# Where the weight tiles of a float32 matmul kernel begin in SBUF, modulo 64 bytes

## What is computed

```python
def _swiglu(h, w_gate, w_up, w_down):
    return (jax.nn.silu(h @ w_gate) * (h @ w_up)) @ w_down

proj = jnp.einsum("bld,de->ble", h, w_in)               # first block, 1024 x 7168
conv_out = jnp.einsum("blc,cd->bld", cu * silu(z_c), w_conv_out)
...
for layer in range(2):
    x = x + 0.5 * _swiglu(_rmsnorm(x, g[0]), ...)       # w_gate, w_up 1024 x 2816
    h = _rmsnorm(x, g[1])
    mix = conv_rwkv_mixer(h, ...) if layer == 0 else mla_mixer(h, ...)
    x = x + mix
    x = x + 0.5 * _swiglu(_rmsnorm(x, g[2]), ...)       # w_down 2816 x 1024
```

## The kernel before, in words

| tiles | begin, modulo 64, before |
|---|---|
| `w_raw`, `w_hi`, `w_lo`, `xT`, `R`, `par`, `ident`, `ones`, `bones` | 0 |
| `gu_w_hi1`, `gu_w2` with `gu_w_lo2` (over the ring) | 0 |
| `gu_w_hi0`, `gu_w0`/`gu_w_lo0`, `gu_w1`/`gu_w_lo1` (in the arena) | 32 |
| all moving tiles of the large products, `tmp`, `st_hi`, `st_lo` | 32 |

## Time and profile before

### The profile page before, as it was taken

How to read it: one execution, slowest core, us unless ns; L and a number is a source line. 1 busy time by engine, 2 the same in 40 slices (tenths; PEclk the granted TensorE clock), 3 DMA queues, 4 the chain that set the end, 5 groups by cost and what they waited for, 6 DMA issues and landing times.

```text
span 2443.8 us, 42260 instructions
## 1 busy us (share of the span) xinstructions
PE 2379.5 (97%) x16963; PEld 2001.1 (82%) x16963; DVE 1738.9 (71%) x2296; ACT 1148.6 (47%) x1758; POOL 879.2 (36%) x533
## 2 busy tenths in 40 slices
PE   8999999999999999989999999999999999999999
PEld 6666767789899777877998998998987557898997
DVE  6999986496485589766864867855846676883771
ACT  5533353465364346244652645643644344662552
POOL 3799934322313456422123123132134212114123
PEclk9999999999999999999999999999999999999999
DMA  5222224233343432002434342342423221333333
GB/s 149 78 78 78 74 65 130 60 93 104 99 111 84 112 93 67 27 4 57 121 84 115 104 121 78 92 124 79 111 85 98 51 57 53 87 94 108 102 89 94
DMA packets 420791, 214.48 MB, mean 88 GB/s; under 512 B 17317, under 2 KB 419035, under 8 KB 420603
## 3 DMA queue, kind: packets, MB, share of 16 engines
q1 hardware_dynamic: 416523, 209.05, 31.1%
q10 hardware_dynamic: 4080, 2.83, 0.5%
HBM read 209.22 MB, written 2.10 MB: 86 GB/s over the span
## 4 chain that ended last, share of the span: by engine, by line
PE 85%; DVE 9%; ACT 3%; issue 2%; POOL 1%; DMA 0%; ACTq 0%; DVEq 0%; POOLq 0%
PE bank L337 11%; PE bank L334 11%; PE bank L330 11%; PE bank L987 11%; PE bank L992 10%; PE bank L995 10%; PE bank L1848 3%; PE bank L1852 3%; PE bank L1855 3%; DVE bank L1682 3%; PE bank L3392 1%; PE bank L2740 1%; PE bank L3458 1%; DVE hL L361 1%; PE bank L2720 1%
## 5 line engine op out<-in xcount | busy, mean ns | idle before, releaser
L312 POOL TENSOR_TENSOR w_lo<-w_raw,w_hi 128x1024 fp32r<-128x1024 f32 (+5 forms) x276 | 532.4, 1931 | 631.9 <-ACT w_hi L304 630.2
L304 ACT ACTIVATE w_hi<-w_raw 128x1024 fp32r<-128x1024 f32 (+5 forms) x276 | 237.7, 861 | 649.0 <-PE bank L337 486.4
L584 DVE TENSOR_TENSOR gu_w_lo<-gu_w,gu_w_hi 128x1024 fp32r<-128x1024 f32 (+1 forms) x256 | 365.2, 1429 | 99.6 <-ACT gu_w_hi L575 99.0
L656 POOL TENSOR_TENSOR ffn_aL<-tmp,ffn_aH 128x512 fp32r<-128x512 f32 x88 | 134.6, 1529 | 739.5 <-ACT ffn_aH L700 739.5
L575 ACT ACTIVATE gu_w_hi<-gu_w 128x1024 fp32r<-128x1024 f32 (+1 forms) x256 | 303.2, 1186 | 3.0 <-DVE gu_w L558 3.0
L692 ACT ACTIVATE tmp<-bank 128x256 f32<-128x256 f32 x320 | 121.6, 380 | 191.0 <-PE bank L995 187.5
L987 PE MATMUL bank<-hH,gu_w_hi 128*128 128x256 f32 x1280 | 205.1, 282 | 4.8 <-ACT tmp L692 4.8
L992 PE MATMUL bank<-hL,gu_w_hi 128*128 128x256 f32 x1280 | 204.0, 282 | 0.0
L995 PE MATMUL bank<-hH,gu_w_lo 128*128 128x256 f32 x1280 | 204.0, 282 | 0.0
L960 DVE TENSOR_TENSOR bank<-bank,R 128x512 f32<-128x512 f32 x64 | 44.8, 699 | 212.9 <-PE bank L337 212.0
L330 PE MATMUL bank<-ffn_aH,w_hi 128*128 128x512 f32 x704 | 185.2, 395 | 0.0
(11 more groups left out here) (553 smaller groups left out, 4707.7 us busy)
## 6 DMA issues: line engine op xcount, KB each, us to landing
gu_w<-in_ffn_w_gate SPq DMA_DIRECT2D x88, 512.0 KB, 4.0
gu_w<-in_ffn_w_up SPq DMA_DIRECT2D x88, 512.0 KB, 5.3
w_raw<-in_w_in SPq DMA_DIRECT2D x48, 512.0 KB, 3.8
w_raw<-in_ffn_w_down SPq DMA_DIRECT2D x64, 384.0 KB, 3.4
w_raw<-in_ffn_w_down SPq DMA_DIRECT2D x64, 320.0 KB, 3.2
w_raw<-in_even_w_in SPq DMA_DIRECT2D x26, 512.0 KB, 3.8
w_raw<-in_w_conv_out SPq DMA_DIRECT2D x8, 512.0 KB, 3.8
w_raw<-in_w_out SPq DMA_DIRECT2D x8, 512.0 KB, 3.8
```

The source lines that it names most:

```text
L304: nc.scalar.activation(w_hi[u % 2][:, 0:K, :], w_raw[u % 4][:, 0:K, :], ACT.Identity).then_inc(w_hi_ready, 1)
L312: nc.gpsimd.tensor_tensor(w_lo[u % 2][:, 0:K, :], w_raw[u % 4][:, 0:K, :], w_hi[u % 2][:, 0:K, :].bitcast(F32), ALU.subtract).then_inc(w_l ...
L584: nc.vector.tensor_tensor(gu_wl[v % 3][:, b0:b1, :, :], gu_w[v % 3][:, b0:b1, :, :], gu_wh[v % 2][:, b0:b1, :, :].bitcast(F32), ALU.subtra ...
L656: nc.gpsimd.tensor_tensor(aL[:, in_half(n), :], up_t[:, :], aH[:, in_half(n), :].bitcast(F32), ALU.subtract).then_inc(a_lo, 1)
```

## The change

Layout only. The 32-byte tile `small` moves to the front, so that `xT`, the ring, `R`, `par` and the constants begin 32 bytes past a multiple of 64; `tmp`, `hH`, `hL` and the arena stay where they were. The gate and up buffers in the arena are moved on by 32 bytes with a new method `skip`, and those laid over the ring begin 32 bytes behind its start, so that all five begin on multiples of 64; `ffn_aH` and `ffn_aL` move by 64 bytes, the `st_` tiles by 128. Shapes, streams of instructions, waits and DMAs are the same.

```diff
@@ -90,11 +90,16 @@
+            def skip(self, n):
+                self.at += n
+                return self.at
+
 ...
         m = Map(base0)
+        small = m.put("small", [P, 8])
         xT = m.put("xT", [P, DT, T])
         ring_at = m.at
 ...
         bones = m.put("bones", [P, P])
-        small = m.put("small", [P, 8])
         tmp = [m.put(f"tmp{i}", [P, T]) for i in range(6)]
@@ -395,15 +399,17 @@
         f_map = Map(ARENA)
-        u_at = [f_map.at, 0, ring_at]
+        u_at = [f_map.skip(32), 0, ring_at + 32]
         f_map.put("gu_room0", [P, 7, 4, P])
+        f_map.skip(32)
         aH = f_map.put("ffn_aH", [P, GU, T], F32R)
         aL = f_map.put("ffn_aL", [P, GU, T], F32R)
-        u_at[1] = f_map.at
+        u_at[1] = f_map.skip(32)
         f_map.put("gu_room1", [P, 7, 4, P])
         gu_w = [Map(at).put(f"gu_w{i}", [P, 7, 4, P]) for i, at in enumerate(u_at)]
         gu_wl = [Map(at).put(f"gu_w_lo{i}", [P, 7, 4, P], F32R) for i, at in enumerate(u_at)]
-        gu_wh = [f_map.put("gu_w_hi0", [P, 7, 4, P], F32R), Map(ring_hi_at).put("gu_w_hi1", [P, 7, 4, P], F32R)]
+        gu_wh = [f_map.put("gu_w_hi0", [P, 7, 4, P], F32R), Map(ring_hi_at + 32).put("gu_w_hi1", [P, 7, 4, P], F32R)]
+        f_map.skip(32)
```

## The result

The changed kernel takes 2431.68 us (median of 4 runs, 2430.86 to 2434.25) where the kernel before, in the 4 runs it has by now, takes 2445.80. The ratio is 0.9942 (95% interval 0.9930 to 0.9954). So it is faster, as forecast, but by 14.1 us and not by 35, and the time lies above the range of 2400 to 2424 us.

What follows compares the result with a forecast made beforehand. TensorE, busy 97% of the span, was taken as the bound. Ring 26.4 plus gate and up 12.1, less plain units 1.8 and waits 1.5, gave 35.2 us: 2443.8 - 35.2 = 2408.6 us, range 2400 to 2424.

Steps and rivals of the forecast that it cites:

- That TensorE bounds, and that a start address sets its spacing: Whole kernel: TensorE, busy 97% of the span, is the bound, and where its weights lie sets a matmul's time.
- The rule for the spacing: Weights at 32 modulo 64 cost 6.6 ns less than at 0 for 512 columns; for 256 columns the sign turns.
- Down halves: Ring units of the eight down halves, 512 columns: 59.8 instead of 61.6 us each, 13.9 us gained.
- The first rival: Down matmuls stay at 233.3 ns if the pair must agree modulo 128: 2422.5 us; 0.10, shared with other missing gains.
- Gate and up: The 80 units of 256 columns, weights moved to 0 modulo 64: all take 9.81 us, 12.1 us gained.
- The third rival: New gate and up residues make the kernel slower, up to 2473.7 us if a bad pair adds 6.6 ns; chance 0.05.
- Ring outside the down halves, less the waits: First block and mixers, ring at 32 modulo 64: 12.5 us gained, 1.5 taken off for waits, 11.0 together.
- Pair loop worth nothing, other engines worth nothing: First block's pair loop, where VectorE never rests, and other engines' tiles with new residues: zero taken for each.
- Plain units: Eight units of 512 columns: 272 matmuls have weights moved from 32 to 0, 1.8 us lost.
- The second rival: Memory region of the weight buffers, ring or arena, sets the rate, so nothing changes: 2443.8 us; chance 0.09.
- The rule against the change: TensorE's two independent read ports never wait, so spacing cannot hang on start addresses; the gain would be zero.
- Nothing has to be carried over: Whole kernel: profiled span 2443.8 us and median run 2443.76 agree, so a sum against the span needs no adjustment.

Runs made afterwards that it cites:

- bare loop: Kernel's work replaced by rows of 32 fp32r matmuls at varied weight and moving-tile starts, nothing else running: 226.7 to 234.3 ns (512 columns), 113.3 to 120.2 (256).
- ring alone: Kernel before with only the ring tiles moved, to 160 modulo 256; gate and up buffers and moving tiles keep their places: 2425.17 us, ratio 0.9922.
- gate and up alone: Changed kernel with the ring back at 128 modulo 256, gate and up buffers placed as in the change: 2444.20 us, ratio 0.9997 to the kernel before.
- the kernel with all weights at 128: Changed kernel with `ffn_aH`, `ffn_aL` back at 160 and all gate and up weights at 128 modulo 256, ring at 160: 2412.71 us, ratio 0.9872.

## Why the prediction was wrong in size

- **That TensorE bounds, and that a start address sets its spacing**: right. A gain of 16.0 us in its busy time became 14.7 us of span.
- **The rule for the spacing: the step that failed.** "High weights and rest both lie at 32 modulo 64, like the moving tiles" took the smallest period that fits the rows. The rows held only weights at 128 and at 160, so they fit modulo 64 and modulo 256 equally, and the bare loop shows that it is the difference of the two starts modulo 256. The rates read at weights 128 and 160 were right, and were then carried to starts where they had not been measured.
- **Down halves**: sized at 13.9 us, measured 3.5. The first rival named this pair, (160, 224), as the one that would fail, with a period of 128 where the bare loop has 256; it had the halves unchanged, and two of the eight took 60.46 us, five 61.49 and the last, with transposes in it, 62.60 for 63.32. The argument against that rival, from `yH`, was no argument: `yH` at 96 has difference 32, whose rate is by chance that of 224.
- **Gate and up**: sized at 12.1 us, measured 1.5. "All units should take the 9.81 us of v = 5" carried the rate of weights at 128 to weights at 0 and 192. The third rival saw that no row has such a pair, and gave it a price on the slow side; the new pairs turned out neither better nor worse. With these buffers at 128 the term is 12.2 us, measured. Of what is missing, 0.9 us lie in the units v = 2 of the third and fourth SwiGLU, which took 14.97 and 15.02 us for 14.53 and 14.55. In the third the wait is as before (2.40 for 2.38 us), but from 1520 to 1545 us the granted clock is 0.93, where before it was 1.00.
- **Ring outside the down halves, less the waits**: 12.5 - 1.5 = 11.0 forecast, 3.1 + 7.9 = 11.0 measured. That the two agree to the tenth is luck: with the same ring the other kernels gained 8.7 (ring alone), 11.8, 8.4 and 7.2 us in these stages, and at least 1.7 of the 7.9 go with the granted clock. The 144 matmuls on `yH` didn't gain, 1 us, which is within what the other items leave.
- **Pair loop worth nothing, other engines worth nothing**: right. The last scan of `z_im` starts at 285.7 us in both traces, and the median rounding of line 575, now 581, takes 1060 ns for 1061.
- **Plain units**: 1.8 us lost forecast, 1.3 measured, but only in part for the reason given. With the ring alone, where their weights did not move, they lost 1.1 us; with gate and up alone 0.6. Some 0.6 of the 1.3 us is waiting: in the fourth SwiGLU TensorE waits 1.34 us for ScalarE's copy into `hH`, where it waited 0.76.
- **The second rival**, the region: refuted by the kernel with all weights at 128. **The rule against the change**: the rows of after again have one form of matmul at 226 and at 233.8 ns by its addresses. The Trainium skill, page "SBUF — State Buffer", section "Who interferes with whom", has two independent read ports and no waiting for TensorE; by it the bare loop would show one spacing for each width. It shows 226.7 to 234.3 and 113.3 to 120.2, with nothing else running, so here the measurement decides against it.

- **"Nothing has to be carried over"**: not so, but small. A run's time lies 1.8 us above its span (2430.86 against 2429.1 us), so the forecast of 2408.6, made from a span, stands for a time of about 2410.4 us (an estimate from these two).

Taken with the rates now known, both misses follow: two terms were read from one pair and spent on another. The range was too narrow for the same reason: it held the first rival but not the first rival together with the gate and up term missing, though both rested on the same unproved period.

**What stays open.** In the changed kernel the down halves of the first SwiGLU hold 229 ns and the others go over to 233.3 at their third unit, at the same addresses. The bare loop had only 229 for this difference at 512 columns, so what tips it wasn't reproduced. Why the spacing hangs on the difference at all (what meets what inside the memory or the engine) wasn't tried. In the kernel with gate and up alone the mixers took 2.1 us more than before, with the ring's places unchanged; that wasn't followed up.

## What to carry to other kernels

Where TensorE bounds a kernel of fp32r matmuls, write down for each kind of matmul the start of the weights less the start of the moving tile, modulo 256, and read its rate from start to start in the timeline: here difference 0 was best for 512 columns (226.7 ns), and 32 below the moving tile was the good one that held for 256 columns (116.7). For 256 columns a start 8 bytes above the moving tile gave 115.8 in the bare loop and wasn't tried in the kernel. Before a rule of layout is extrapolated, ask which periods the rows can tell apart; if they can't, either move only into pairs that the trace already shows, or time the pairs in a bare loop first. A tile moved to keep its own alignment changes every pair that it is in, so list them all.

## What the runs showed of the hardware that was not expected

- The period is 256 bytes, and the difference counts: eight absolute places agreed within 0.2 ns for seven of eight differences at 512 columns and for three of eight at 256, where others have more than one rate.
- Starts less than 32 bytes apart matter too: 226.7, 230.7 and 233.4 ns for 0, 8 and 16 bytes at 512 columns.
- Even the best pair leaves 226.7 - 213.3 = 13.4 ns over the time of 512 columns at 2.4 GHz.
- One pair can have two steady spacings (113.3 and 117.8 ns for 256 columns and difference 64), held over a whole unit of 84 matmuls. In the kernel the slower one was the usual, so the fastest number of a bare loop is not what a kernel gets.
